# Attention values with the values as weights and the probabilities as 512 moving columns; some weight splits on GpSimd

## The reference

```python
xn = rms_norm(h, norm_g); proj = xn @ w_in
mixed = concat([ya * silu(ga), yb * silu(gb), yc * silu(gc)])
h = h + mixed @ w_out
```

```python
mx = maximum(max(s), sink); pr = exp(s - mx)
denom = sum(pr) + exp(sink - mx)
o = einsum('bnkgqs,bnskd->bnqkgd', pr / denom, v_all)
```

## Time and profile before

| | us |
|---|---|
| median of the runs | 1633.67 |
| the profiled execution | 1633.94 |
| its span, first to last instruction | 1632.2 |
| PE busy | 1611.1 (99%) |
| DVE busy | 915.8 (56%) |
| ACT busy | 645.5 (40%) |
| POOL busy | 20.7 (1%) |

### The profile page before, as it was taken

The page is one execution under the profiler, slowest core; times in us unless marked ns, Lnnn a source line. Parts: engine busy times, 40 slices in busy tenths (PEclk is TensorE's granted clock), DMA queues, the critical chain, the costliest instruction groups (busy, mean ns, idle before and its releaser), DMA issues.

```text
span 1632.2 us, 27854 instructions
## 1 busy us (share of the span) xinstructions
PE 1611.1 (99%) x11366; PEld 1491.8 (91%) x11366; DVE 915.8 (56%) x1897; ACT 645.5 (40%) x1280; POOL 20.7 (1%) x78
## 2 busy tenths in 40 slices
PE   6999999999999999999999999999999999999999
PEld 6999999999999999999998899889999978888887
DVE  7677877645666554434335678774555674443231
ACT  7676455423222432323237764553223233232121
POOL 0000000000000000000000000000000000000000
PEclk9999999999999999999999999999999999999999
DMA  6222211112121222434342221111212112233341
GB/s 251 84 100 78 79 35 45 53 53 78 53 78 53 82 100 89 147 120 154 119 142 79 103 78 53 53 52 53 78 52 78 68 63 97 84 130 134 139 155 65
DMA packets 28014, 147.23 MB, mean 90 GB/s; under 512 B 3568, under 2 KB 3696, under 8 KB 12656
## 3 DMA queue, kind: packets, MB, share of 16 engines
q1 hardware_dynamic: 27888, 145.46, 25.4%
HBM read 136.86 MB, written 8.52 MB: 89 GB/s over the span
## 4 chain that ended last, share of the span: by engine, by line
PE 96%; DVE 2%; issue 1%; ACT 0%; DMA 0%; SPq 0%; DVEq 0%
PE ps_gemm L798 80%; PE ps_mix L688 3%; PE ps_mix L724 3%; PE ps_mix L640 2%; PE ps_mix L654 2%; PE ps_mix L683 1%; PE ps_gemm L616 1%; DVE rstd L883 1%; PE ps_mix L768 1%; PE ps_mix L770 0%; PE ps_mix L700 0%; PE ps_mix L757 0%; PE ps_mix L719 0%; DVE w_lo L865 0%; DMA w_stage<-in_w_in 0%
## 5 line engine op out<-in xcount | busy, mean ns | idle before, releaser
L798 PE MATMUL ps_gemm<-x_hi,w_hi 128*128 128x264 f32 (+1 forms) x2304 | 561.2, 311 | 13.5 <-DVE w_lo L865 10.9
L798 PE MATMUL ps_gemm<-x_hi,w_lo 128*128 128x264 f32 (+1 forms) x2304 | 542.7, 303 | 0.0
L798 PE MATMUL ps_gemm<-x_lo,w_hi 128*128 128x264 f32 (+1 forms) x2304 | 542.0, 303 | 0.0
L798 PEld LDWEIGHTS ps_gemm<-x_hi,w_hi 128*128 128x128 f32 x2304 | 370.6, 189 | 34.1 <-DVE w_lo L865 12.0
L798 PEld LDWEIGHTS ps_gemm<-x_hi,w_lo 128*128 128x128 f32 x2304 | 370.4, 189 | 16.4
L798 PEld LDWEIGHTS ps_gemm<-x_lo,w_hi 128*128 128x128 f32 x2304 | 369.8, 188 | 14.4
L865 DVE TENSOR_TENSOR w_lo<-w_stage,w_hi 128x512 fp32r<-128x512 f32 x464 | 305.6, 690 | 103.9 <-ACT w_hi L422 92.4
L422 ACT ACTIVATE w_hi<-w_stage 128x512 fp32r<-128x512 f32 x464 | 265.4, 618 | 169.7 <-DVE z L943 122.8
L798 PE MATMUL ps_gemm<-mixed_hi,w_lo 128*128 128x264 f32 (+1 forms) x768 | 205.2, 322 | 0.0
L798 PE MATMUL ps_gemm<-mixed_lo,w_hi 128*128 128x264 f32 (+1 forms) x768 | 205.0, 321 | 0.0
L798 PE MATMUL ps_gemm<-mixed_hi,w_hi 128*128 128x264 f32 (+1 forms) x768 | 203.8, 320 | 0.0
(11 more groups left out here) (169 smaller groups left out, 1407.4 us busy)
## 6 DMA issues: line engine op xcount, KB each, us to landing
w_stage<-in_w_in SPq DMA_DIRECT2D x83, 1024.0 KB, 4.8
w_stage<-in_w_out SPq DMA_DIRECT2D x32, 1024.0 KB, 5.2
x_in<-in_xT SPq DMA_DIRECT2D x4, 1056.0 KB, 9.9
res<-in_xT SPq DMA_DIRECT2D x16, 264.0 KB, 5.3
h1T<-z SPq DMA_DIRECT2D x16, 264.0 KB, 5.7
res<-h1T SPq DMA_DIRECT2D x16, 264.0 KB, 5.2
out<-z SPq DMA_DIRECT2D x16, 256.0 KB, 5.5
rope<-in_c_rope SPq DMA_DIRECT2D x2, 528.0 KB, 4.7
```

The costliest lines, as they stand in the source:

```text
L798: ins = pe.matmul(g[:, bank, 0:size], ws, xs[:, k, c:c + size], start=tick == 0 and i == 0, stop=tick == TICKS - 1 and i == 2)
```

## The change

1. The value matmul is turned around. The values of a key block, as weights 128 keys x 128 columns, hold their high parts in the 64 columns of the own head and the low parts in the other 64 (`vs`). The transposed probabilities of the four heads, split in high and low (`pth`, `ptl`), are 512 moving columns. So there are 4 fp32r matmuls for b of 2 or more, 2 for b = 1, and one for the meta keys (`vm` against `bd`). The result is transposed already; `outputs_t` goes. ACT copies the half with the low parts to SBUF (`ol`), DVE adds the halves into `y` (64 x 512 elements).
2. The division is put off: the denominators are collected in `den`, inverted once, transposed by PE, written to DRAM, loaded back repeated over 64 partitions (`rdb`), and eight DVE products in slots 23 and 25 (tick 6) apply them to `y`.
3. New on DVE: the low parts of the probabilities (128 x 512 elements for a pair of heads, half of that for b = 1), a product of 128 x 4 x 128 elements in place of the copy L1081, the low parts of the values in slot 2. New on GpSimd: a subtraction beside each L408. In `vm` eight DMAs in place of four and a memset.
4. `w_low` of slots 12 to 20 runs on GpSimd instead of DVE.
5. Cells are spread over the ticks otherwise: 1.0 tick a cell for the lead and b = 0, 1.6 for b = 1, 1.9 for b of 2 or more, 1.2 for the last 17. All ends in slot 20 or earlier.

```diff
-EXP_LAG, PAIR_LAG, META_LAG, VALUE_LAG, OUT_LAG = 4, 6, 9, 11, 13
+EXP_LAG, PAIR_LAG, META_LAG, VALUE_LAG, OUT_LAG = 4, 6, 9, 11, 12
+RECIP_LAG, RECIP_T_LAG, RECIP_OUT_LAG = 14, 15, 16
+CELL_TICKS = {0: 1.0, 1: 1.6, 2: 1.9, 3: 1.9, 4: 1.9}
+LEAD_TICKS, TAIL_TICKS, TAIL_CELLS = 1.0, 1.2, 17
+RECIP_LOAD_SLOTS, RECIP_SLOTS, RECIP_TICK = (22, 24), (23, 25), 6
+WLO_POOL = range(ATT_SLOT + 1, 21)
...
+                if n == RECIP_LOAD_SLOTS[0]:
+                    rows = 4 * len(ATT_B[layer])
+                    sp.wait_ge(s_rde, layer + 1)
+                    sp.dma_start(rdD[0:rows], rdt[0:rows]).then_inc(s_rdo, 16)
+                    sp.wait_ge(s_rdo, 16 * (layer + 1))
+                    load_recips(layer, 1)
+                if n == RECIP_LOAD_SLOTS[1]:
+                    sp.wait_ge(s_rdm, 8 * layer + 4)
+                    load_recips(layer, 0)
...
+            def w_low(N, q):
+                pool.wait_ge(s_whi, 4 * N + q + 1)
+                ks = slice(4 * q, 4 * q + 4)
+                pool.tensor_tensor(wl[:, N % 3, ks], wst[:, N % 3, ks], wh[:, N % 2, ks].bitcast(F32), ALU.subtract)\
+                    .then_inc(s_wlp, 1)
+            def probs_meta(layer, q, pair):
...
+                pool.tensor_copy(pmc[0:nq, Q % 2, 0, heads], src).then_inc(s_apc, 1)
+                pool.wait_ge(s_apc, 2 * Q + pair + 1)
+                pool.tensor_tensor(pmc[0:nq, Q % 2, 1, heads], src, pmc[0:nq, Q % 2, 0, heads].bitcast(F32),
+                                   ALU.subtract).then_inc(s_apm, 1)
...
                 if no:
-                    pe.wait_ge(s_ape, no)
+                    pe.wait_ge(s_apl, no)
...
-                o = M[0:nq, 3, 0:256]
-                last = pe.matmul(o, pmt[0:64, 0:nq], vm[0:64, kv].rearrange("p i d -> p (i d)"),
-                                 start=True, stop=b == 0)
+                o = M[:, 3, 0:4 * nq]
+                last = pe.matmul(o, vm[:, kv], bd[:, :, 0:nq], start=True, stop=b == 0)
                 if b:
-                    for i in range(4):
-                        for s in range(0 if b >= 2 else 1, 2):
-                            last = pe.matmul(o[:, DH * i:DH * i + DH], pts[:, i // 2, i % 2, s],
-                                             vb[:, b - 1 + s, DH * kv:DH * kv + DH],
-                                             start=False, stop=i == 3 and s == 1)
+                    for s in range(0 if b >= 2 else 1, 2):
+                        for part in (pth, ptl):
+                            last = pe.matmul(o, vs[:, b - 1 + s, kv], part[:, s].rearrange("p i q -> p (i q)"),
+                                             start=False, stop=s == 1 and part is ptl)
...
+            def att_probs_low(layer, q, pair):
...
+                dve.wait_ge(s_ape, no + 1)
+                signal(dve.tensor_tensor(ptl[:, first:2, heads],
+                                         M[:, 2].rearrange("p (s i q) -> p s i q", s=2, i=2)[:, first:2],
+                                         pth[:, first:2, heads].bitcast(F32), ALU.subtract), s_apl)
...
+                dve.wait_ge(s_aol, Q + 1)
+                signal(dve.tensor_tensor(y[rows, 4 + 4 * j:8 + 4 * j, blk(b)],
+                                         M[rows, 3, 0:4 * nq].rearrange("p (i q) -> p i q", i=4),
+                                         ol[rows, 0:4 * nq].rearrange("p (i q) -> p i q", i=4), ALU.add), s_aod)
...
+            def att_apply_recips(layer, j):
+                c = slice(0 if layer == 0 else N_META, T)
+                dve.wait_ge(s_rdi, recip_loads(layer, 2 - j))
+                for i in range(4):
+                    m = 4 + 4 * j + i
+                    signal(dve.tensor_tensor(y[:, m, c], y[:, m, c], rdb[:, i, c], ALU.mult), s_rdm)
```

More of the change, by code:

```diff
@@ L117 @@
 AT_META, AT_CUR, BAND = P, P + N_META, 2 * P + N_META
+N_CST = P + BAND + NG * PAD + 4
 KB = N_META + P
@@ L297, in att_at @@
         def att_at(layer, n, tick, lag):
-            job = att_job(n, tick)
+            job = att_job(layer, n, tick)
             if job is None:
@@ L315, in att_pair_at @@
         def att_pair_at(layer, n, tick, job):
-            now = att_job(n, tick)
+            now = att_job(layer, n, tick)
             if now is None:
@@ L391, in _ @@
         def _(pool):
[L392 to L409, removed]
+            def w_low(N, q):
[4 more added lines that the diff above has]
+            def probs_meta(layer, q, pair):
+                Q = ATT_Q0[layer] + q
+                nq = N_META if ATT_B[layer][q][0] == 0 else P
+                heads = slice(2 * pair, 2 * pair + 2)
+                src = pr[0:nq, Q % 2, heads, AT_META:AT_CUR]
+                if Q >= 2:
+                    pool.wait_ge(s_amt, Q - 1)
+                pool.wait_ge(s_aex, 4 * Q + 2 * pair + 2)
+                pool.tensor_copy(pmc[0:nq, Q % 2, 0, heads], src).then_inc(s_apc, 1)
+                pool.wait_ge(s_apc, 2 * Q + pair + 1)
+                pool.tensor_tensor(pmc[0:nq, Q % 2, 1, heads], src, pmc[0:nq, Q % 2, 0, heads].bitcast(F32),
+                                   ALU.subtract).then_inc(s_apm, 1)
+            for N in range(NTOT):
+                layer, n = divmod(N, NC)
+                for tick in range(TICKS):
+                    if tick - 1 in HI_TICKS and N + 1 < NTOT and low_on_pool(N + 1):
+                        w_low(N + 1, HI_TICKS.index(tick - 1))
+                    at = att_at(layer, n, tick, EXP_LAG)
+                    if at and at[1] % 2 == 1:
+                        probs_meta(layer, at[0], at[1] // 2)
         @block.scalar
@@ L825, in _ @@
                         probs_t(layer, at[0], at[1] // 2)
-                    at = att_at(layer, n, tick, OUT_LAG)
-                    if at and at[1] == 0 and ATT_B[layer][at[0]][2] == 1:
-                        outputs_t(layer, at[0])
+                    at = att_at(layer, n, tick, RECIP_T_LAG)
+                    if at and at == (len(ATT_B[layer]) - 1, 0):
+                        recips_t(layer)
                     h, r = hgrn_at(n, tick)
@@ L1214, in _ @@
                         pooling_last(N - 1)
-                    if tick - 1 in HI_TICKS and N + 1 < NTOT:
+                    if tick - 1 in HI_TICKS and N + 1 < NTOT and not low_on_pool(N + 1):
                         w_low(N + 1, HI_TICKS.index(tick - 1))
```

206 lines of the change are left out of this document (135 added, 71 removed).

## The result

The changed kernel takes 1657.6 us (median of 4 runs, 1654.7 to 1660.3) against 1633.7 for the kernel before on the same chip: ratio 1.0147, 95% interval 1.0134 to 1.0159. It is slower by 24 us. I had said 1600 with a range of 1585 to 1624, and 5% for slower. The profiled execution took 1660.27 us; its span is 1658.5.

The account below looks back on a forecast made before the run. PE, busy 99% of the span, was taken to bound the kernel. Its stream 50.6 us shorter gives 1583.1; adding 3 (DVE over), 3 (bursts), 7 (lock) and 3.6 (slot 25) gives 1599.7, called 1600, range 1585 to 1624.

Parts of the forecast that it names:

- The turned matmul: PE's new value matmuls in the attention: 0.231 us each for 512 columns, 0.39 as upper bound.
- `w_low` on GpSimd: Weight subtractions of slots 12 to 20, 72 in all: 1.3 us each, upper bound 3.4 us.
- reciprocals that are not late: Slots 22 to 25: nothing late unless the 512-byte rows land over 8 us after their issue.
- the hold of the lock on VectorE: GpSimd's `w_low` delaying VectorE's instructions with two SBUF inputs: 2 us a slot at most.
- The 1.8 us in slot 25: PE waits 1.8 us for a level behind the products on VectorE, in each layer; 3.6 us in all.
- the sum: Whole kernel: 1583.1 + 3 (DVE over) + 3 (bursts) + 7 (lock) + 3.6 = 1599.7 us, given as 1600.
- 93 to 95%: VectorE's real load in slots 13 and 14 of the kernel before, uncounted gaps included, with PE waiting for nothing.
- DVE, per slot: Attention slots: VectorE's work against PE's in each slot, the excess becoming PE time, 3 us u slots, 3 us gates.
- The second step: Lock between GpSimd and VectorE: 1.2 us of PE time in six u slots, 7 us; hidden in gate slots.
- PE alone: Whole kernel, PE's stream 50.6 us shorter and nothing else counted: 1633.7 - 50.6 = 1583.1 us.
- rival (d): Slower than before: the lock with a `w_low` from about 3 us on GpSimd, 63 us, 1646 us; chance 0.05.
- Rival (c): VectorE the bound throughout: 18 slots lose the full 2 us, or the matmul costs 0.39; 1612 to 1633 us; chance 0.15.

Follow-up runs that it names:

- low_first: Changed kernel with VectorE's low half of a probability pair placed ahead of the meta take-out and mask of its cell; 1642.3 us.
- values_tick: Changed kernel with PE issuing `values`, and the transposition of a first pair behind it, one tick later; 1633.6 us.
- no_wlo: Changed kernel without the weights' low halves in slots 12 to 20, PE taking the high half in their place; 1631.7 us.
- wlo_dve: Changed kernel with the weights' low halves of slots 12 to 20 back on VectorE; 1658.5 us.

## Why the prediction was wrong

**Right in their sizes.** The turned matmul at 0.231 us (measured 0.235), `w_low` on GpSimd at 1.3 us (mean 1.34, 72 times), L700 gone, reciprocals that are not late, and the hold of the lock on VectorE: "2 us of DVE a slot at most", 36 us in 18 slots, and 28 to 34 were measured. GpSimd's group (after; shapes, count, busy us, mean ns):
```profile
L460 POOL TENSOR_TENSOR w_lo<-w_stage,w_hi 128x512 fp32r<-128x512 f32 x72 | 96.1, 1339 | 892.2 <-ACT w_hi L497 891.9
```
The 1.8 us in slot 25 came as worked out from the earlier trace rows. The products stand between `w_low` and the next level, and PE waits 1.82 us for it, in PE's and VectorE's order of time (after):
```profile
434.20 0.69 DVE L950 TENSOR_TENSOR w_lo<-w_stage,w_hi 128x512 fp32r<-128x512 f32 x1
434.81 2.93 DVE L1220 TENSOR_TENSOR y<-y,a_rden 128x528 f32<-128x528 f32 x4
437.78 0.43 DVE L1253 COPY_PREDICATED h_att<-level_mask,ps_mix 96x256 f32<-96x256 uint8 x1
```
```profile
439.48 0.65 PE L808 MATMUL ps_mix<-h_qp,h_k 128*64 128x64 f32 x8 [1.82 <-DVE h_k L1269]
```
PE's waits for this tile rose from 1.3 to 4.8 us in all, 3.5 for the 3.6 of the sum.

Two figures of the prediction are misworked, and the sum uses neither. VectorE at "93 to 95%" in slots 13 and 14 should read 97 and 94%: 15.78 and 17.36 us with 53 and 51 gaps of 0.04, of 18.40 and 20.60. And the Trainium skill's 4497 ns for 2048 elements ("GPSIMD Engine Reference", section "Elementwise — side-by-side cycle accounting") scale to an estimated 1.1 us for 512, not 1.2; this case's trace has 1.34.

**The step that failed** is the one headed "DVE, per slot". It set VectorE's work in a slot against PE's work in the same slot, 18.2 against 16.6 us, 19.0 against 19.2, and took the excess, 1.6, 0.9 and a little for bursts, as the wait: 3 + 3 us. That bounds the wait from below only, for it lets VectorE work ahead in one cell and make up in another. The kernel doesn't allow it: a mask waits for the scores of its own cell, `values` for the low half of the cell before. The sum has to be made from one hand-over to the next, 6.4 us of VectorE against 5.6 of PE, and the 2.84 us in which it idles behind `values` don't count. I did name the new waits (`probs_t` for the low parts one cell back), but `values` comes ahead of `probs_t` in the tick and needs the same low half, so the wait came there, at 30 of 32 groups: 41.5 us for the 6 of the sum. It is shown by the two runs that change only a place: low_first −15.3 and values_tick −24.0 us, with VectorE busy 957.1 and 958.3 us, against 957.3. They don't bring back all that was lost, and the second step has its share.

**The second step** is the lock: 7 us, with "in the gate slots DVE has 2 us to spare, and it is hidden". The hold was sized well, its effect was not. The same hold, spread over all slots, lands on a path that has nothing to spare: 10 us slower in the kernel before, which has no wait of PE in the attention, and 26 us between the changed kernel and `no_wlo`. `wlo_dve` gives the balance: 50 us of VectorE's work taken away, 32 put back by the lock, time unchanged.

**What the sum didn't have.** The profiled execution took 1660.3, 77.2 us above the 1583.1 of PE alone. Waits for the low half 41.5; their restarts, 0.24 us each, 31 times, 7; other new waits in the attention (scores for masks and queries 2.4 and 1.1, `values` for the output's adding 1.4) 5; slot 25, 3.5; the clock, at 0.992 instead of 1.000, 13. That makes 70; 7 us are spread over differences too small to name. The clock was no item of mine at all: the kernel before has 1.000 over the whole span. These terms are read from the trace and the mean clock; no run takes the clock or the restarts away by themselves.

The rival (d), slower, had the right sign and in part the right mechanism, but priced it for a `w_low` of 3 us and over. With 1.34 it was enough, because it wasn't alone. Rival (c), VectorE the bound throughout, fits no view: VectorE is busy 81% of slot 14 and idles 2.84 and 3.64 us in the stretch shown.

## What to carry over

When work moves onto an engine that feeds the bottleneck, don't add it up per stage: follow one round of the pipeline from hand-over to hand-over and compare the two engines' work between them, in their program order. An idle share of 10 to 20% in such a loop is no reserve, since it may all lie behind the deadline. The helper that takes the work can also hold up the feeder: here GpSimd's passes, 90 to 96 us of them, held VectorE some 30. Before taking work off the feeder, look at what stands ahead of the awaited instruction in its own program: an instruction whose inputs are ready should not be queued behind one that waits for the bottleneck.

## What the runs showed of the hardware

**The lock holds small and single-input instructions too, and not those that read PSUM.** VectorE's groups by shape (after; busy us, mean ns):
```profile
L1186 DVE TENSOR_TENSOR a_pt_lo<-ps_mix,a_pt_hi 128x512 fp32r<-128x512 f32 x48 | 33.2, 691 | 10.4 <-ACT a_pt_hi L646 8.9
...
L1153 DVE TENSOR_SCALAR att_stat<-att_stat 128x4 f32<-128x4 f32 x32 | 10.4, 324 | 3.8 <-DVE att_stat L1149 0.5
...
L1364 DVE TENSOR_TENSOR a_q_stack<-y,a_q_stack 64x512 fp32r<-64x512 f32 x32 | 26.1, 815 | 1.1
```
The same groups of `no_wlo`:
```profile
L1186 DVE TENSOR_TENSOR a_pt_lo<-ps_mix,a_pt_hi 128x512 fp32r<-128x512 f32 x48 | 33.2, 692 | 10.4 <-ACT a_pt_hi L646 8.9
...
L1153 DVE TENSOR_SCALAR att_stat<-att_stat 128x4 f32<-128x4 f32 x32 | 5.5, 170 | 3.8 <-DVE att_stat L1149 0.5
...
L1364 DVE TENSOR_TENSOR a_q_stack<-y,a_q_stack 64x512 fp32r<-64x512 f32 x32 | 22.0, 686 | 1.1
```
A statistic of four columns takes 324 instead of 170 ns on average, because six of the 32 last 0.9 to 1.0 us and end just behind a `w_low` that was under way; the low half of the probabilities, with one input in PSUM, takes 691 and 692. The Trainium skill has this rule in "SBUF — State Buffer" (section "SBUF: two separate sides"): whichever of the two engines starts first gets the shared pair of ports for its whole instruction; of VectorE's instructions it concerns those with two SBUF inputs and those in a mode that uses two ports. The trace agrees for both directions now, 1.75 us for a product of 0.71 here and 0.74 for a copy of 0.21 in the earlier trace rows.

**A short stop of PE can cost as much again in clock.** PE stands 2.69 us up to 242.39. In the stretch from 240 to 245 us it is busy 2.61 us, and the granted clock falls to 0.77 of full, that is, part of it at the lower level of 1.2 GHz. The chain of waits (after) has the new matmuls at half speed there:
```profile
242.39 0.47 PE ps_mix L772
242.85 1.69 PE ps_mix L776 x4
244.55 0.85 PE ps_mix L744 x4
```
That is 0.42 us for a matmul and 0.21 for a transposition, against 0.235 and 0.11 in the chain at 254.67. Behind the 1.82 us of slot 25 it is the same (after, by windows): the clock falls to 0.66 in the five microseconds that follow the wait, although PE is busy in all of them.
```profile
435.00:440.00 5.00, 3.18 (x31) 2.99 (x30) 4.67 (x9) 0.00 (x0) 0.00 (x0) 1.00 0.00 0
440.00:445.00 5.00, 5.00 (x32) 4.95 (x29) 2.26 (x6) 0.00 (x0) 0.00 (x0) 0.66 0.01 3
```
Not every stop does it, and not the same stop in every kernel. Before the wait of 0.99 us at 253.2 and after it the matmuls run at full speed. In `values_tick` PE stands the same 1.82 us in slot 25, up to 426.96, and the clock stays full (values_tick, by windows):
```profile
425.00:430.00 5.00, 3.18 (x30) 3.00 (x29) 4.52 (x11) 0.00 (x0) 0.00 (x0) 1.00 0.02 3
430.00:435.00 5.00, 5.00 (x45) 5.00 (x44) 1.97 (x5) 1.76 (x3) 0.00 (x0) 1.00 0.23 57
```
In `no_wlo`, with as many waits for the low half (30) but none longer than 2.0 us, the clock is 0.999. What decides whether a stop costs clock is not shown by these runs.
